# Regrouping the matrix engine's work in the RWKV part of a two-layer decoder step: whole v pieces, two transposing steps moved, new order strings

## What is computed

```python
r = xr @ w_r; k = xk @ w_k; v = xv @ w_v
a = sigmoid(a0 + (xa @ a1) @ a2)
kk = k * k_k;  kk = kk / max(sqrt(sum(kk * kk, per head)), 1e-12)
k = k * (1 + (a - 1) * k_a)
# per token, state S (64 x 64) per head, w the decay:
Sa = S @ (-kk);  S = S * w + Sa (x) (kk * a) + v (x) k;  y = S @ r
y = group_norm(y) * gn_g + gn_b + (sum(r * k * r_k)) * v
out = (y * g) @ w_o
```

## The kernel before

| step | what it does |
|---|---|
| D1 to D4 | weight pieces 0 to 3 (k): each 4 tiles x 3 passes = 12 matmuls of 128x288; D4 also the first low-rank product (3) |
| D5 | second low-rank product, then piece 5 (v, first of four) |
| D6 to D11 before | pieces 6, 7, 8 (v) in halves of 6 matmuls (`half`); the key norm (kn, L851) follows the second half of piece 6, in D7; D12 is empty |
| F1, F2 | norm sums (L791, L794: two 128x288 records each); F1 also transposes the sample states (s0, L889) |
| F3 (tok) | transposes the features (L903, 8 of 128x128), then the samples' (L908, 64x64) |
| F4 (prod) | products of the features; F5 is empty |
| F6, F8, F10 (x0, x1, x2) | first product of a level (L870, 64x64 blocks); VectorE masks it (L1919), for x1 ScalarE also copies three tiles (L1423 to L1425) |
| F7, F9, F11 (t0, t1, t2) | second product of a level; VectorE adds it and transposes (L1927, L1846), for t2 it also makes two more tiles (L1929, L1939) |
| B1 to B4 | x3, t3, x4, t4; x4 (L870) is followed by the transposes of the samples' updates (L951, four of 128x128) |
| B5, B6 | q; then state 0 (64x64) and products with 128 rows and 64 columns of the array (L1000) |
| B7 to B12 | u1, s1, u2, s2, u3, s3: the state from block to block; u is L1007, s is L991 and L993; VectorE answers with L1964 and L1969 |
| B13 (fin) | turns the final state (L879) |

## Time and profile before

### The profile page before, as it was taken

The page is one execution under the profiler, slowest core; times in us unless marked ns, Lnnn a source line. Parts: engine busy times, 40 slices in busy tenths (PEclk is TensorE's granted clock), DMA queues, the critical chain, the costliest instruction groups (busy, mean ns, idle before and its releaser), DMA issues.

```text
span 2710.4 us, 56335 instructions
## 1 busy us (share of the span) xinstructions
PE 2595.7 (96%) x23289; PEld 2482.9 (92%) x23289; DVE 1564.6 (58%) x2331; ACT 1147.5 (42%) x1660; POOL 142.2 (5%) x211
## 2 busy tenths in 40 slices
PE   7989999999998899999999999968999999999997
PEld 6988888888788899999999999958999999999997
DVE  7887778778855644444444444586444444444446
ACT  4565555555533533333333333345333333333334
POOL 1001111111000100000000000100000000000000
PEclk9999999999999899999999999979999999999999
DMA  7532223222335665556665556524665556555553
GB/s 227 158 87 78 74 76 83 78 83 78 94 95 160 166 171 161 165 143 169 185 170 160 166 142 169 176 78 112 168 168 159 148 163 187 168 167 161 146 164 95
DMA packets 707050, 379.29 MB, mean 140 GB/s; under 512 B 16023, under 2 KB 699191, under 8 KB 706711
## 3 DMA queue, kind: packets, MB, share of 16 engines
q1 hardware_dynamic: 701040, 363.42, 47.9%
q0 software_dynamic: 5792, 13.34, 1.8%
q10 hardware_dynamic: 70, 0.39, 0.1%
HBM read 367.28 MB, written 10.62 MB: 139 GB/s over the span
## 4 chain that ended last, share of the span: by engine, by line
PE 84%; DVE 10%; ACT 4%; issue 2%; DMA 1%; DVEq 0%; SPq 0%; POOL 0%; ACTq 0%
PE PS L708 25%; PE PS L709 24%; PE PS L710 24%; PE PS L870 3%; DVE WL L1677 2%; ACT WH L1245 1%; ACT L1372 1%; DVE TM L1685 1%; DVE ML L1692 1%; PE PS L918 1%; PE PS L903 1%; DVE TM L1824 1%; PE PS L940 1%; PE PS L725 1%; PE PS L946 0%
## 5 line engine op out<-in xcount | busy, mean ns | idle before, releaser
L1677 DVE TENSOR_TENSOR WL<-RAW,WH 128x2048 fp32r<-128x2048 f32 (+1 forms) x325 | 658.6, 2027 | 763.2 <-ACT WH L1245 763.2
L708 PE MATMUL PS<-MH,WH 128*128 128x288 f32 (+1 forms) x3152 | 933.4, 296 | 24.5 <-DVE ML L2079 11.3
L709 PE MATMUL PS<-ML,WH 128*128 128x288 f32 (+1 forms) x3152 | 934.8, 297 | 0.0
L710 PE MATMUL PS<-MH,WL 128*128 128x288 f32 (+1 forms) x3152 | 933.9, 296 | 0.0
L1245 ACT ACTIVATE WH<-RAW 128x2048 fp32r<-128x2048 f32 (+1 forms) x325 | 553.3, 1703 | 821.6 <-PE PS L710 808.5
L708 PEld LDWEIGHTS PS<-MH,WH 128*128 128x128 f32 (+1 forms) x3152 | 596.5, 189 | 30.7 <-issue 19.8
L709 PEld LDWEIGHTS PS<-ML,WH 128*128 128x128 f32 (+1 forms) x3152 | 596.8, 189 | 0.2
L710 PEld LDWEIGHTS PS<-MH,WL 128*128 128x128 f32 (+1 forms) x3152 | 596.0, 189 | 0.0
L709 PE MATMUL PS<-HL,WH 128*128 128x288 f32 x1408 | 415.3, 295 | 0.0
L710 PE MATMUL PS<-HH,WL 128*128 128x288 f32 x1408 | 415.0, 295 | 0.0
L708 PE MATMUL PS<-HH,WH 128*128 128x288 f32 x1408 | 413.4, 294 | 0.0
(11 more groups left out here) (304 smaller groups left out, 2695.0 us busy)
## 6 DMA issues: line engine op xcount, KB each, us to landing
RAW<-in_ffn_w_in SPq DMA_DIRECT2D x176, 1024.0 KB, 5.6
RAW<-in_ffn_w_down SPq DMA_DIRECT2D x128, 704.0 KB, 4.8
RAW<-in_rw_wr SPq DMA_DIRECT2D x16, 1024.0 KB, 6.0
PR<-in_rw_wk SPq DMA_DIRECT2D x64, 256.0 KB, 2.7
PR<-in_rw_wv SPq DMA_DIRECT2D x64, 256.0 KB, 2.8
PR<-in_rw_wo SPq DMA_DIRECT2D x64, 256.0 KB, 3.2
S0N<-in_state_wkv POOLq DMA_DIRECT2D x64, 64.0 KB, 2.3
out<-SOS POOLq DMA_DIRECT2D x64, 64.0 KB, 2.5
```

What stands on the lines that cost most here:

```text
L708: pe.matmul(out, wh, xh, start=first, stop=False)
L709: pe.matmul(out, wh, xl, start=False, stop=False)
L710: return pe.matmul(out, wl, xh, start=False, stop=last)
L1677: dve.tensor_tensor(WL[0:rows, j % 2, 0:n], RAW[0:rows, j, 0:n], WH[0:rows, j % 2, 0:n].bitcast(F32), ALU.subtract).then_inc(lo_ready, 1)
```

## The change

1. `half` goes: pieces 6, 7 and 8 of v are whole steps of 12 matmuls. DENSE on TensorE has 9 steps (D1 to D5 as before, D6, D7, D8 for pieces 6, 7, 8, D9 empty). The key norm follows piece 7 (D7) instead of piece 6.
2. In tok (F3) the samples' 64x64 matmuls come ahead of the eight 128x128 transposes.
3. The transposes of the samples' updates come ahead of x4's 64x64 blocks in B3, and so their wait for the updates (snw2) too.
4. All three order strings are new. Nothing is computed otherwise, and the DMAs are the same.

```diff
-        ORDER = {"pe": "FDBDFBFDBFBDFFBDFBDFBDFBDFBDFBDBBDBD", "dve": "FBFDFDBDBDFBFFFBDFBDFBDFBDDFBDFBBBDBD",
-                 "act": "DFBDFBDFDBFBDFFBDDFBFBDFBFBDDFBBBBDDB"}
+        ORDER = {"pe": "FDBDFBFDBFBDFFBDBFBDBFBFBDBFBDFBD", "dve": "FBFDFDBDBDFBFFFBDBFBDBFBFBDDBFBBDFDDD",
+                 "act": "DFBDFBDFDBFBDFFBDDBFBBFBFBBDDDFBBDDFB"}
...
-                    def half(bank, j, k0, part, xh, xl):
...
                     for j in range(6, 9):
-                        half(D1, j, 4 * (j - 5), 0, MH[0], ML[0])
-                        yield
-                        half(D1, j, 4 * (j - 5), 1, MH[0], ML[0])
-                        if j == 6:
+                        columns(D1, j, 4 * (j - 5), MH[0], ML[0])
+                        if j == 7:
                             ready(z.dact, "a")
                             z.dpe.done(pe.matmul(D0[:, 0:T], HEADS, z.YT, start=True, stop=True), "kn")
                         yield
...
-                    for t in range(2):
-                        for n, f in enumerate(feats):
-                            pe.transpose((PA, PB)[t][:, n * P:(n + 1) * P], f[:, t * P:(t + 1) * P], IDN)
                     for h in range(2):
...
-                            ins = pe.matmul(PC[q, T + n * HN:T + (n + 1) * HN], f, CP[q, q], start=True, stop=True)
+                            pe.matmul(PC[q, T + n * HN:T + (n + 1) * HN], f, CP[q, q], start=True, stop=True)
+                    for t in range(2):
+                        for n, f in enumerate(feats):
+                            ins = pe.transpose((PA, PB)[t][:, n * P:(n + 1) * P], f[:, t * P:(t + 1) * P], IDN)
...
+                    if lv == 4:
+                        await_step(z.dve, "snw2", i)
+                        for b in range(4):
+                            pe.transpose(PA[:, b * P:(b + 1) * P], z.UVX[:, 2 * b:2 * b + 2, :], IDN)
                     await_step(z.dve, f"turn{lv - 1}" if lv else "turn", i)
...
-                    if lv == 4:
-                        await_step(z.dve, "snw2", i)
-                        for b in range(4):
-                            ins = pe.transpose(PA[:, b * P:(b + 1) * P], z.UVX[:, 2 * b:2 * b + 2, :], IDN)
...
-            weave("D" * PHASES[DENSE], pair, (0, 0, DENSE))
+            weave("D" * 9, pair, (0, 0, DENSE))
```

## The result

The changed kernel takes 2749.02 us (median of 4 runs, 2746.54 to 2756.4) against 2710.51 us for the kernel before on the same chip; the ratio is 1.0146, with a 95% interval of 1.0126 to 1.0166, or 39.6 us. The forecast was 2736.5 with a range up to 2750: the sign and the mechanism came as told, the size was 12.5 us short, some 7 of them in the clock's term. Its mean clock is 0.974, where it was 0.985.

A forecast was written before the change was run, and what follows sets the result against it. TensorE was taken to set the pace of the RWKV pass's turns. Turns +8.4, first unit +2.6 and start +1.6 made +12.6 us; with the clock's 13.5, +26.1 on 2710.28: 2736.5 us, range 2718 to 2750.

The forecast's parts named there:

- the clock's term: TensorE falls to half clock behind D1's stops: 15 stops give 10 spells, 1.35 us lost in each, +13.5 us.
- D1 waits for piece 0: Between turns TensorE's D1 stops for piece 0, made by VectorE behind t2's work: +2.6 us a turn (2.2 to 3.0).
- t1 waits for x1: On TensorE t1 waits for x1's mask and copy, with only u2's two matmuls as cover: +0.56 us a turn.
- The stop in front of u3: TensorE's regular wait ahead of u3 goes, as a whole piece now stands in front: 1.1 us a turn saved.
- Crossings: Stretches of 128x128 matmuls between 64x64 work on TensorE fall from 13 to 8: net 1.45 us a turn saved.
- A steady turn: A turn of the RWKV pass at full clock goes from 36.05 to 36.66 us; 14 turns make +8.4 us.
- The key norm: At the start, chunk 0's DENSE has it behind piece 7, 12 matmuls later, delaying the path: +1.6 us.
- The first unit: Behind the 15th turn the same wait as D1's hits the first output unit: +2.6 us.
- Rival 1: D1's stop comes but the clock stays full: 2723 us, chance 0.17.
- Rival 2: D1's stop is short, so the kernel is faster: 2684 us with no stop, 2698 halfway; chance 0.11.
- Rival 3: On TensorE the regrouping does not save its crossings: 1.45 us a turn come back, +20 us, 2757 us; chance 0.07.
- rival 4: Stop and savings just cancel, leaving the time within 5 us of before; chance 0.05.

## Where the prediction failed, and what of it held

The step that failed is the clock's term (+13.5 us), by its size. I had ten spells in 15 stops, at 1.35 us. There were 12 in the first trace and 13 in the second, two and three of them twice as long, and a spell cost 1.46 or 2.77 us: 17.5 in the 13 turns, 1.46 in the last and some 1.4 behind the unit's stop, 20.4 in all, 7 more than the term. I took the frequency from three rows of other stages, and the price from matmuls lost within 3.4 us. That ten was near the 10 to 13 of three traces is luck. Spells of 6.8 us were in the trace of before too (865.70 to 872.50, shown above); I did not look for them. The mechanism held: D1 waits for piece 0, and the clock falls behind many of these stops. The other terms:

- **D1 waits for piece 0** (+2.6): 2.74 us. The order of the four parts came as worked out, and so did their length: 297.96 to near 301.50 is 3.54 us, for which the sum had 3.53. Of the 0.14 us over the term 0.09 lie between the piece's end (near 301.50) and the matmul (301.64), for which I took 0.05: the trace has the load of D1's first weights at 301.61, behind the wait and not ahead of it. The stop and the clean turn move together through four kernels that differ in VectorE's string alone: no steady stop and 34.69 us, 1.04 and 35.28, 2.50 and 36.74, 3.40 and 37.66.
- **t1 waits for x1** (+0.56): 325.30 to 325.99 is 0.69, with the usual step of 0.06 off 0.63 us.
- **The stop in front of u3** (-1.1): the row is gone. **Crossings** (-1.45): two of the five measured by themselves, 0.22 and 0.30 for 0.33 and 0.29 (in the latter four steps of 0.12 us are 0.48 and not 0.46, which takes 0.02 off it). From the turn's 0.69 = 2.74 + 0.63 - 1.1 - x the net of all five would be 1.6; that is a remainder, which takes u3's 1.1 as forecast, and not a measurement.
- **A steady turn** (36.66): 36.74. 14 of them make +9.7 (13 x 0.69 and 0.7 in the last turn) where the sum had 8.4.
- **The key norm** (+1.6): right in size, as its own experiment shows, but in the first turn and not ahead of it, and it did not show in the comparison, since before had a spell there: the sum had 1.6 us, the ledger has 0.1.
- **The first unit** (+2.6): too small. The tail's string begins with the unit, so F1 does not stand between t2 and it, which I left out. TensorE's timeline in that place:

```profile
758.14 0.49 PE L708 MATMUL PS<-LHH,PH 128*128 128x288 f32 x1 [3.52 <-DVE PL L1754]
758.43 0.44 PE L709 MATMUL PS<-LHL,PH 128*128 128x288 f32 x1
```

  3.5 us, and half clock behind it (records of 0.44 us, where 0.29 is usual).

Together: 9.7 + 3.5 + 20.4 = 33.6 us, and the start, the first turn and the rest, 2.4 us, of which the start's 1.3 vary from trace to trace and the rest was not traced to a cause. The median's 38.5 to 39.6 us go beyond the profiled execution's 35.9; the executions differ, and by the clock too: that of 2746.54 us had a mean clock of 0.977, that of 2756.4 us 0.972.

The upper end of the range was too high by its own terms: a stop of 3.0 us and 12 spells give 14 x 1.0 + 3.0 + 1.6 + 12 x 1.35 = 34.8 us, which is 2745 and not 2750. So that 2749.02 lies below 2750 is not to the sum's credit.

Rival 1 (the clock stays, 2723) fell: the kernel with the stop and the clock of that rival would be the fourth turn, 36.75 us, and only three of 13 turns are like it. The Trainium skill (TensorE: Matmul & The Clock Gate, on oscillation in real kernels) puts the fall of the clock down to idle gaps longer than the change's. The runs disagree: stops of 2.50 us of idle time were followed by a spell in ten of 13 cases. Stops of 3.40 us, in turn, left the clock at full in six of 13. Rival 2 fell as to this change; of its sum (2684 to 2698), the kernel with piece 0 first came within 2 us and those with new strings passed it. Rival 3 (2757) fell with the two crossings measured, the change's busy time and the 34.69 us turn, rival 4 with the time.

Open: what, beside the stop, decides whether the clock falls. The place in time fits the two traces of one program, but nothing here was made to set that place. Stops of 1.04 us never cost it, in 13 cases. Those of about 2 us went both ways: a spell stood behind 2.07 us at 719.36 with the reciprocal first, none behind 2.23 us at 844.85 with piece 0 first; and one stop of 2.05 us in the tail of the change had a spell behind it in the first trace (at 835.24) and none in the second (at 838.51).

## What to carry to other kernels

Where the order of every engine is written by hand, a regrouping on one engine has to be followed by a walk through the other engines' queues: for each step that the busy engine waits for, list what stands ahead of it in its own queue, back to the last thing that came from the busy engine. Here two letters on VectorE, 57% busy, were worth 49 us of 2749. Count a regular stop of the matrix engine twice, once for its length and once for the clock behind it, and take the frequency of the latter as unknown between none and all until a trace shows it.

## What the runs showed of the hardware

- Whether half clock follows a stop is not settled by the stop's length: the same 2.5 us of idle time in the same turn left the clock at 1.00 in one trace and brought 0.50 in the other.
- Longer stops did not bring more spells: nine and nine in 15 stops of 3.40 us or more, ten, twelve and thirteen in 15 stops of 2.50 us or more. Behind 13 stops of 1.04 us there was none.
- Taking a stretch of 128x128 transposes out of 64x64 work saved TensorE 0.22 us (eight transposes) and 0.30 us (four).
- D1 began 0.14 us after the end of the piece that it waited for (near 301.50 and 301.64), t1 0.06 us after the end of its mask (325.93 and 325.99).
